# A mixer stage: attention steps with a second probability buffer and later transposes, and the recurrence's products on VectorE

## The chip, the cores and the metric

The kernel runs on one core of one Trainium2 chip. The metric is the device time of one execution in microseconds. The core has a matrix engine (TensorE, PE), a vector engine (VectorE, DVE), an engine for functions of one operand (ScalarE, ACT), a general engine (GpSimd, POOL), and SyncE, which issues most DMAs. Each works through its own queue in order; semaphores tie the queues together.

## The reference, cut to what matters

One decoder block over 512 tokens of width 1024: a mixer with two parallel groups of heads, then a channel mixer that retrieves experts. The change touches the mixer between its input projection and its output projection:

```python
def one_block(args):                       # differential attention, 4 heads, two maps j each
    s = jnp.einsum('bhjqd,bhjkd->bhjqk', qi, k) * scale
    s = jnp.where(mask, s, -jnp.inf)
    p = jax.nn.softmax(s, axis=-1)
    a = p[:, :, 0] - lam * p[:, :, 1]
    return jnp.einsum('bhqk,bhkv->bhqv', a, vf)

def step(state, inp):                      # HGRN2 recurrence, 4 heads, chunkwise
    q_, k_, v_, b_ = inp                   # b_: running sum of the log of the forget gate
    decay = jnp.exp(jnp.where(causal, b_[..., :, None, :] - b_[..., None, :, :], -jnp.inf))
    attn = jnp.einsum('bhtk,bhtsk,bhsk->bhts', q_, decay, k_)
    o_intra = jnp.einsum('bhts,bhsv->bhtv', attn, v_)
    o_inter = jnp.einsum('bhtk,bhkv->bhtv', q_ * jnp.exp(b_), state)
    ...
```

## The kernel before

The kernel is a row of stages with a barrier between them: input projection, `stage_mix`, `stage_join` (output projection and residual), selection, gates, experts. Everything that the diff touches lies in `stage_mix`. Its operands are in SBUF already; it starts no DMA.

The attention is worked through in 16 steps (`STEPS_A`), step n being head n // 4 and query tile n % 4, so a step has one to four key tiles of 128. A loop over n is written out for each engine, with 18 turns. In turn n

- TensorE forms the scores of step n (L943, and the causal mask by L946) into PSUM banks 2(n % 2) and the next, the product with the values of step n-2 (L955), then in turns 0 to 7 column sums of the modulation (L314) or in turns 8 to 17 eight level products of the recurrence in two groups (L930), and last the transposes of `mixed` of step n-1 (L973);
- VectorE takes the maxima of step n (L840), scales them into `nbias` (L842), and mixes step n-1: reciprocals of the sums and their factor (L850, L851), the first map scaled (L852) and the second added to it (L854), into `mixed`. In the turns of `ITEMS` it subtracts for one level of the recurrence (L862, L875, for the last item L866), and in turns 8 to 17 it copies two groups of level products under a mask (L830);
- ScalarE forms the exponentials of step n into `prob` (L768), copies out the attention of step n-2 (L774), copies the transposes of step n-1 into `mixedT` (L780), squares the attention (L783), and in the turns of `ITEMS` forms the exponentials of a level (L788, L789, L799, L800, L793, L794).

`prob` is one buffer, so exp(n) waits for mix(n-1) (`mixed_ready`); `nbias`, `Z`, `mixed`, `mixedT` and the score banks have two.

The recurrence is split into five levels (`LEVELS`): inside blocks of 8, and between halves of blocks of 16, 32, 64 and 128. For each level the exponentials `E` are multiplied by `kk` and `q` into `F` (L725, L726 for level 0; L736, L737 for the others, half a tile each), and so are those for the carried state (`"kb"`, L741, L742). GpSimd does this, each level as soon as its exponentials are there (`exp_ready`) and its slot of `F` is free (`level_done`). It then multiplies the output gate `hg` by its gain (L743). Ahead of all that it fills masks (L704 to L722).

Behind the loop TensorE transposes `F` slot 3 (L982), ScalarE copies that into `kbT` (L804), TensorE forms the chunk states (L990), VectorE carries them on (L894 to L900), and TensorE forms the recurrence's output (L1001, L1004). GpSimd normalizes the attention meanwhile (L749, L751).

Of the kernel before, what the change touches and what calls it, by code (L numbers as in the profile page):

```python
# [9 lines left out]
ALU = mybir.AluOpType  # L10
ACT = mybir.ActivationFunctionType
AX_X = mybir.AxisListType.X

P = 128
# [600 lines left out]
STEPS_A = HEADS * TT  # L615
LEVEL_AT = 8
LEVEL_END = LEVEL_AT + HEADS * len(LEVELS) // 2

ITEMS = {1: 0, 3: 1, 5: 2, 7: 3, 9: 4, 11: "kb"}
SLOT_E = (0, 0, 1, 0, 1)  # L620
# [3 lines left out]
def stage_mix(nc, a, m):  # L624
    with ExitStack() as own:
# [16 lines left out]
        prob = sb("prob", [P, 2, S])  # L642
# [59 lines left out]
        def _(pool):  # L702
# [21 lines left out]
            pool.wait_ge(exp_ready, 1)  # L724
            g.tensor_tensor(F[:, 0, :], E[:, 0, :], kk, ALU.mult).then_inc(f_ready, 1)  # L725
            g.tensor_tensor(F[:, 1, :], E[:, 1, :], q, ALU.mult).then_inc(f_ready, 1)  # L726
            for level in range(1, len(LEVELS)):
                h = LEVELS[level]
                pool.wait_ge(exp_ready, level + 1)
                if level == 3:  # L730
                    pool.wait_ge(level_done, HEADS)
                out = F[:, SLOT_F[level][0], :].rearrange("p (n c) -> p n c", c=2 * h)
                e = E[:, SLOT_E[level], :].rearrange("p (n c) -> p n c", c=2 * h)
                kv = kk.rearrange("p (n c) -> p n c", c=2 * h)
                qv = q.rearrange("p (n c) -> p n c", c=2 * h)
                g.tensor_tensor(out[:, :, 0:h], e[:, :, 0:h], kv[:, :, 0:h], ALU.mult).then_inc(f_ready, 1)  # L736
                g.tensor_tensor(out[:, :, h:], e[:, :, h:], qv[:, :, h:], ALU.mult).then_inc(f_ready, 1)  # L737

            pool.wait_ge(exp_ready, len(LEVELS) + 1)
            pool.wait_ge(level_done, 3 * HEADS)  # L740
            g.tensor_tensor(F[:, 2, :], E[:, 0, :], q, ALU.mult).then_inc(f_ready, 1)  # L741
            g.tensor_tensor(F[:, 3, :], E[:, 1, :], kk, ALU.mult).then_inc(f_ready, 1)  # L742
# [14 lines left out]
        def _(act):  # L757
# [3 lines left out]
            for n in range(STEPS_A + 2):  # L761
                if n < STEPS_A:
                    k = (n % TT + 1) * P
                    act.wait_ge(bias_ready, n + 1)
                    if n >= 1:
                        act.wait_ge(mixed_ready, n)
                    for j in range(2):
                        A(prob[:, j, 0:k], m.psum[2 * (n % 2) + j][:, 0:k], ACT.Exp, bias=nbias[:, n % 2, j:j + 1],  # L768
                          scale=QK ** -0.5, accum_out=Z[:, n % 2, j:j + 1]).then_inc(probs_ready, 1)
# [1361 lines left out]
```

## Time and profile before

| | |
|---|---|
| Time, median of 3 runs | 1952.97 us (1951.37 to 1954.81) |
| The profiled execution's own time | 1953.12 us |
| Its span | 1951.4 us |
| Mean granted TensorE clock | 0.945 |
| Busy in the span: TensorE, VectorE, ScalarE, GpSimd | 1796.0, 1182.1, 707.6, 672.1 us |
| `stage_mix`'s loop | 214.8 to 346.1 us |

Span is the time from the first to the last instruction. Times of instructions are counted from the span's start. A granted clock of 1.00 is 2.4 GHz, of 0.50 1.2 GHz. On TensorE the product of two fp32 operands shows as several records; "x8" counts records. "Idle before, releaser" in square brackets is how long the engine stood still before an instruction and what ended that. A difference between starts is often more telling than a duration, since the end of one instruction overlaps the start of the next.

### The profile page before, as it was taken

The page shows a single profiled execution, that of the slowest core. Times are in us where ns is not written, and L with a number is a line of the kernel's source. Part 1 is how long each engine was busy: PE and PEld are TensorE (multiplying, and loading weights), DVE is VectorE, ACT ScalarE, POOL GpSimd, SP SyncE. Part 2 cuts the span into 40 slices and gives each one's busy share as a digit, 9 for nine tenths or more (in the row PEclk, how much of TensorE's full clock was granted, in tenths as well). Part 3 has the DMA queues.
Part 4 walks back from the last instruction along what each step waited for, and adds up shares of the span by engine and source line. Part 5 has one row for each costly group of instructions (what it writes and reads, how often), then busy time and mean ns, then how long its engine had stood idle before and what let it go on. Part 6 is the DMA issues. An engine that isn't in the chain of part 4 may idle for free. (4 is left out here: it accounts for less than half of the span.)

```text
span 1951.4 us, 23199 instructions
## 1 busy us (share of the span) xinstructions
PE 1796.0 (92%) x8309; PEld 1482.8 (76%) x8309; DVE 1182.1 (61%) x2038; ACT 707.6 (36%) x1113; POOL 672.1 (34%) x486
## 2 busy tenths in 40 slices
PE   6999886777999689999998999999899999999996
PEld 6877564656777578888887888888688888888885
DVE  3766467734999945545553333333357887778776
ACT  3213343433332235555554223222233333333332
POOL 0000333203867642222221000000166776667750
PEclk8999767897999889999999999999999999999998
DMA  8563000312223234456556655555488988899985
GB/s 352 182 226 108 1 1 1 134 66 92 76 70 115 90 119 157 157 189 192 167 188 204 218 187 182 176 176 191 148 302 298 351 320 323 300 349 359 319 301 196
DMA packets 159708, 369.92 MB, mean 190 GB/s; under 512 B 16288, under 2 KB 78240, under 8 KB 156192
## 3 DMA queue, kind: packets, MB, share of 16 engines
q1 hardware_dynamic: 137120, 302.08, 44.4%
q0 software_dynamic: 22528, 67.19, 9.7%
q8 instruction: 20, 0.33, 0.1%
q14 instruction: 40, 0.33, 0.1%
HBM read 306.30 MB, written 62.91 MB: 189 GB/s over the span
## 5 line engine op out<-in xcount | busy, mean ns | idle before, releaser
L2064 PE MATMUL bank<-hl,actT 128*128 128x512 f32 x2304 | 524.5, 390 | 9.8 <-DVE actT L2004 9.8
L2064 PEld LDWEIGHTS bank<-hl,actT 128*128 128x128 f32 x2304 | 433.3, 188 | 101.0 <-DVE hl L1999 11.0
L1788 PE MATMUL bank<-actT,hl 128*128 128x512 f32 x1440 | 329.5, 391 | 6.8 <-DVE hl L1759 6.8
L1788 PEld LDWEIGHTS bank<-actT,hl 128*128 128x128 f32 x1440 | 272.3, 189 | 63.7 <-DVE hl L1759 7.0
L1644 PE MATMUL bank<-actT,hl 128*128 128x512 f32 x1152 | 275.5, 395 | 6.2 <-DVE hl L1603 6.2
L1644 PEld LDWEIGHTS bank<-actT,hl 128*128 128x128 f32 x1152 | 214.2, 189 | 48.7 <-DVE hl L1603 6.4
L1424 PE MATMUL bank<-actT,hl 128*128 128x512 f32 x864 | 212.3, 405 | 31.4 <-POOL hl L1270 28.1
L1961 ACT ACTIVATE hl<-v_raw 128x1024 fp32r<-128x1024 f32 x128 | 135.6, 1059 | 285.7 <-PE bank L2064 259.1
L1920 POOL DMA_INDIRECT rows<-in_v,own_index x65 | 83.6, 1286 | 422.8 <-POOLq L1684 351.9
L1424 PEld LDWEIGHTS bank<-actT,hl 128*128 128x128 f32 x864 | 167.3, 196 | 70.4 <-POOL hl L1270 18.5
L1999 DVE TENSOR_TENSOR hl<-v_raw,hl 128x1024 fp32r<-128x1024 f32 x128 | 157.1, 1227 | 90.1 <-ACT hl L1961 89.8
L1926 POOL DMA_INDIRECT own_act<-early_activations,own_at x128 | 180.6, 1411 | 39.1 <-issue 39.1
L1542 POOL TENSOR_TENSOR onehot<-first_hits,slotsT 128x512 f32<-128x512 bf16 x48 | 91.2, 1901 | 261.2 <-DVE first_hits L1610 261.2
L1768 DVE TENSOR_TENSOR kept_acts<-kept_acts,group_gates 128x384 f32<-128x384 f32 x60 | 33.5, 558 | 174.5 <-ACT kept_acts L1742 124.8
L1571 ACT ACTIVATE onehot<-first_hits,slotsT 128x128 f32<-128x128 bf16 x192 | 85.2, 515 | 78.7 <-DVE first_hits L1610 78.7
L1603 DVE TENSOR_TENSOR hl<-raw,hl 128x1024 fp32r<-128x1024 f32 x48 | 58.8, 1226 | 89.2 <-ACT hl L1557 89.2
L1270 POOL TENSOR_TENSOR hl<-raw,hl 128x1024 fp32r<-128x1024 f32 x32 | 82.0, 2564 | 81.3 <-ACT hl L1290 81.3
L1742 ACT ACTIVATE kept_acts<-bank 128x512 f32<-128x512 f32 x60 | 35.8, 597 | 201.8 <-PE bank L1788 201.8
L1759 DVE TENSOR_TENSOR hl<-raw,hl 128x1024 fp32r<-128x1024 f32 x60 | 73.3, 1226 | 55.7 <-ACT hl L1733 55.7
L1920 POOL DMA_INDIRECT raw<-in_v,own_index x63 | 77.6, 1232 | 54.8 <-DVE raw L2020 21.4
L1660 PEld LDWEIGHTS bank<-onehot 128*128 128x128 f32 x768 | 93.1, 191 | 3.7
L1660 PE MATMUL bank<-onehot 128*128 128x128 f32 x768 | 93.4, 275 | 0.0
(254 smaller groups left out, 2291.0 us busy)
## 6 DMA issues: line engine op xcount, KB each, us to landing
raw<-in_u SPq DMA_DIRECT2D x128, 512.0 KB, 3.8
v_raw<-in_v SPq DMA_DIRECT2D x128, 512.0 KB, 6.0
expert_gates<-gates SPq DMA_DIRECT2D x12, 2048.0 KB, 9.8
group_gates<-expert_gates SPq DMA_DIRECT2D x32, 768.0 KB, 6.2
acts_in<-early_activations SPq DMA_DIRECT2D x100, 192.0 KB, 4.9
wada<-in_w_ada SPq DMA_DIRECT2D x9, 2048.0 KB, 7.5
early_activations<-kept_acts SPq DMA_DIRECT2D x60, 256.0 KB, 2.2
early_activations<-gate_acts SPq DMA_DIRECT2D x48, 256.0 KB, 2.3
```

The costliest lines, as they stand in the source:

```text
L1270: g.tensor_tensor(hl[:, 1, u % m.split, :], raw[:, u, :], hl[:, 0, u % m.split, :].bitcast(F32), ALU.subtract).then_inc(m.unit_lo, 1)
L1424: last = nc.tensor.matmul(m.psum[u % 2][:], hl[:, x, u % m.split, kc * P:(kc + 1) * P], m.actT[:, z, kc, :], start=(kc == 0 and j == 0), s ...
L1542: nc.gpsimd.tensor_tensor(onehot1[:, b % BUFS, 0:pool_n, :].rearrange("p t k -> p k t"), hits[:, b % BUFS, :, 0:pool_n], slotsT[:, 2, n].u ...
L1571: last = A(onehot1[:, r % BUFS, u, :], hits[:, r % BUFS, :, u], ACT.Copy, scale=slotsT[:, 2, at:at + 1])
L1644: last = nc.tensor.matmul(m.psum[n % 2][:], hl[:, x, n % m.split, kc * P:(kc + 1) * P], m.actT[:, z, kc, :], start=(kc == 0 and j == 0), s ...
L1660: last = nc.tensor.matmul(chunk_bank(b, c)[:, k * NKEY:(k + 1) * NKEY], onehot1[:, b % BUFS, u, :], onehot2[:, b % BUFS, u, :], start=True ...
L1788: last = nc.tensor.matmul(m.psum[u % 2][:], hl[:, x, u % m.split, kc * P:(kc + 1) * P], m.actT[:, z, kc, :], start=(kc == 0 and j == 0), s ...
L1920: nc.gpsimd.indirect_dma_start(out=fetched[k % FETCH], out_offset=None, in_=rows_of_v, in_offset=bass.IndirectOffsetOnAxis(ap=m.own_index[ ...
L1926: nc.gpsimd.indirect_dma_start(out=own_act[:, k:k + 1], out_offset=None, in_=acts_of_u, in_offset=bass.IndirectOffsetOnAxis(ap=m.own_at[:, ...
L1961: A(v[:, 0, j, :], v_raw[:, j, :], ACT.Copy).then_inc(v_hi, 1)
L1999: V.tensor_tensor(v[:, 1, j, :], v_raw[:, j, :], v[:, 0, j, :].bitcast(F32), ALU.subtract).then_inc(v_lo, 1)
L2064: last = nc.tensor.matmul(bank(t, half)[:], w[:, x, j, t * P:(t + 1) * P], v[:, z, j, half * S:(half + 1) * S], start=(first and j == 0 an ...
```

## The change

`prob` becomes two buffers, and exp(n) waits for mix(n-2) instead of mix(n-1). TensorE transposes step n-2 instead of n-1 in turn n and forms the values' product of step n-3 instead of n-2; ScalarE's copies follow; the loop has 19 turns. The twelve products into `F` leave GpSimd's queue and go into VectorE's, at the turns that `PRODUCTS` lists, behind the mix and ahead of `ITEMS` and of the masked copies. GpSimd keeps the masks and, right behind them, the product of `hg` with its gain.

```diff
--- before.py
+++ after.py
@@ -613,10 +613,12 @@
 CHUNK = P
 NCH = S // CHUNK
 STEPS_A = HEADS * TT
+LAST = 3
 LEVEL_AT = 8
 LEVEL_END = LEVEL_AT + HEADS * len(LEVELS) // 2
 
 ITEMS = {1: 0, 3: 1, 5: 2, 7: 3, 9: 4, 11: "kb"}
+PRODUCTS = {2: (0,), 4: (1,), 6: (2,), 10: (3, 4), 14: ("kb",)}
 SLOT_E = (0, 0, 1, 0, 1)
 SLOT_F = ((0, 1), (2, 2), (3, 3), (0, 0), (1, 1))
 
@@ -639,7 +641,7 @@
         attnT = sb("attnT", [P, HEADS, S])
         kbT = sb("kbT", [P, NCH - 1, HEADS * HD])
         state = sb("state", [P, NCH - 1, HEADS * HD])
-        prob = sb("prob", [P, 2, S])
+        prob = sb("prob", [P, 2, 2, S])
         mixed = sb("mixed", [P, 2, S])
         mixedT = sb("mixedT", [P, 2, S])
         masks = sb("masks", [P, len(LEVELS), P])
@@ -721,25 +723,6 @@
                                                   pattern=[[2 * h, P // (2 * h)], [0, h]], channel_multiplier=-1))
             g.memset(attnT[:], 0.0).then_inc(masks_ready, 1)
 
-            pool.wait_ge(exp_ready, 1)
-            g.tensor_tensor(F[:, 0, :], E[:, 0, :], kk, ALU.mult).then_inc(f_ready, 1)
-            g.tensor_tensor(F[:, 1, :], E[:, 1, :], q, ALU.mult).then_inc(f_ready, 1)
-            for level in range(1, len(LEVELS)):
-                h = LEVELS[level]
-                pool.wait_ge(exp_ready, level + 1)
-                if level == 3:
-                    pool.wait_ge(level_done, HEADS)
-                out = F[:, SLOT_F[level][0], :].rearrange("p (n c) -> p n c", c=2 * h)
-                e = E[:, SLOT_E[level], :].rearrange("p (n c) -> p n c", c=2 * h)
-                kv = kk.rearrange("p (n c) -> p n c", c=2 * h)
-                qv = q.rearrange("p (n c) -> p n c", c=2 * h)
-                g.tensor_tensor(out[:, :, 0:h], e[:, :, 0:h], kv[:, :, 0:h], ALU.mult).then_inc(f_ready, 1)
-                g.tensor_tensor(out[:, :, h:], e[:, :, h:], qv[:, :, h:], ALU.mult).then_inc(f_ready, 1)
-
-            pool.wait_ge(exp_ready, len(LEVELS) + 1)
-            pool.wait_ge(level_done, 3 * HEADS)
-            g.tensor_tensor(F[:, 2, :], E[:, 0, :], q, ALU.mult).then_inc(f_ready, 1)
-            g.tensor_tensor(F[:, 3, :], E[:, 1, :], kk, ALU.mult).then_inc(f_ready, 1)
             g.tensor_tensor(hg.rearrange("p (n c) -> p n c", c=HD), hg.rearrange("p (n c) -> p n c", c=HD),
                             g_hgrn.unsqueeze(1).to_broadcast([P, TT * HEADS, HD]), ALU.mult).then_inc(hg_ready, 1)
 
@@ -758,28 +741,28 @@
             A = nc.scalar.activation
             act.wait_ge(lam_sums, 1)
             A(lams[:, 2:4], lams[:, 0:2], ACT.Exp).then_inc(lam_exps, 1)
-            for n in range(STEPS_A + 2):
+            for n in range(STEPS_A + LAST):
                 if n < STEPS_A:
                     k = (n % TT + 1) * P
                     act.wait_ge(bias_ready, n + 1)
-                    if n >= 1:
-                        act.wait_ge(mixed_ready, n)
+                    if n >= 2:
+                        act.wait_ge(mixed_ready, n - 1)
                     for j in range(2):
-                        A(prob[:, j, 0:k], m.psum[2 * (n % 2) + j][:, 0:k], ACT.Exp, bias=nbias[:, n % 2, j:j + 1],
+                        A(prob[:, n % 2, j, 0:k], m.psum[2 * (n % 2) + j][:, 0:k], ACT.Exp, bias=nbias[:, n % 2, j:j + 1],
                           scale=QK ** -0.5, accum_out=Z[:, n % 2, j:j + 1]).then_inc(probs_ready, 1)
-                if n >= 2:
-
-                    h, t = divmod(n - 2, TT)
-                    act.wait_ge(attn_out, n - 1)
+                if n >= 3:
+
+                    h, t = divmod(n - 3, TT)
+                    act.wait_ge(attn_out, n - 2)
                     A(cat[:, t, h * HD:(h + 1) * HD], m.psum[5][:, 0:HD], ACT.Copy).then_inc(attn_read, 1)
-                if 1 <= n <= STEPS_A:
-                    k = ((n - 1) % TT + 1) * P
-                    act.wait_ge(mixed_tr, n)
-                    if n >= 3:
-                        act.wait_ge(attn_out, n - 2)
-                    A(mixedT[:, (n - 1) % 2, 0:k], m.psum[4][:, 0:k], ACT.Copy).then_inc(mixedT_ready, 1)
-                if n >= 2:
-                    act.wait_ge(attn_read, n - 1)
+                if 2 <= n < STEPS_A + 2:
+                    k = ((n - 2) % TT + 1) * P
+                    act.wait_ge(mixed_tr, n - 1)
+                    if n >= 4:
+                        act.wait_ge(attn_out, n - 3)
+                    A(mixedT[:, n % 2, 0:k], m.psum[4][:, 0:k], ACT.Copy).then_inc(mixedT_ready, 1)
+                if n >= 3:
+                    act.wait_ge(attn_read, n - 2)
                     m.act.then(act, A(squared[:], cat[:, t, h * HD:(h + 1) * HD], ACT.Square,
                                       accum_out=ss[:, 0, t, h:h + 1]))
                 item = ITEMS.get(n)
@@ -832,7 +815,29 @@
                                       m.psum[6 + u % 2][:].rearrange("p (n c) -> p n c", c=P)
                                       ).then_inc(level_copied, 1)
 
-            for n in range(STEPS_A + 2):
+            def products(level):
+                if level == 0:
+                    dve.wait_ge(exp_ready, 1)
+                    V.tensor_tensor(F[:, 0, :], E[:, 0, :], kk, ALU.mult).then_inc(f_ready, 1)
+                    V.tensor_tensor(F[:, 1, :], E[:, 1, :], q, ALU.mult).then_inc(f_ready, 1)
+                elif level == "kb":
+                    dve.wait_ge(exp_ready, len(LEVELS) + 1)
+                    dve.wait_ge(level_done, 3 * HEADS)
+                    V.tensor_tensor(F[:, 2, :], E[:, 0, :], q, ALU.mult).then_inc(f_ready, 1)
+                    V.tensor_tensor(F[:, 3, :], E[:, 1, :], kk, ALU.mult).then_inc(f_ready, 1)
+                else:
+                    h = LEVELS[level]
+                    dve.wait_ge(exp_ready, level + 1)
+                    if level == 3:
+                        dve.wait_ge(level_done, HEADS)
+                    out = F[:, SLOT_F[level][0], :].rearrange("p (n c) -> p n c", c=2 * h)
+                    e = E[:, SLOT_E[level], :].rearrange("p (n c) -> p n c", c=2 * h)
+                    kv = kk.rearrange("p (n c) -> p n c", c=2 * h)
+                    qv = q.rearrange("p (n c) -> p n c", c=2 * h)
+                    V.tensor_tensor(out[:, :, 0:h], e[:, :, 0:h], kv[:, :, 0:h], ALU.mult).then_inc(f_ready, 1)
+                    V.tensor_tensor(out[:, :, h:], e[:, :, h:], qv[:, :, h:], ALU.mult).then_inc(f_ready, 1)
+
+            for n in range(STEPS_A + LAST):
                 if n < STEPS_A:
                     k = (n % TT + 1) * P
                     dve.wait_ge(scores, n + 1)
@@ -849,10 +854,12 @@
                         dve.wait_ge(mixed_tr, o - 1)
                     m.dve.then(dve, V.reciprocal(rz[:, o % 2, :], Z[:, o % 2, :]))
                     m.dve.then(dve, V.tensor_scalar(rz[:, o % 2, 1:2], rz[:, o % 2, 1:2], lams[:, 0:1], None, ALU.mult))
-                    m.dve.then(dve, V.tensor_scalar(mixed[:, o % 2, 0:k], prob[:, 0, 0:k], rz[:, o % 2, 0:1], None,
+                    m.dve.then(dve, V.tensor_scalar(mixed[:, o % 2, 0:k], prob[:, o % 2, 0, 0:k], rz[:, o % 2, 0:1], None,
                                                     ALU.mult))
-                    V.scalar_tensor_tensor(mixed[:, o % 2, 0:k], prob[:, 1, 0:k], rz[:, o % 2, 1:2],
+                    V.scalar_tensor_tensor(mixed[:, o % 2, 0:k], prob[:, o % 2, 1, 0:k], rz[:, o % 2, 1:2],
                                            mixed[:, o % 2, 0:k], ALU.mult, ALU.add).then_inc(mixed_ready, 1)
+                for level in PRODUCTS.get(n, ()):
+                    products(level)
                 item = ITEMS.get(n)
                 if item is not None:
                     if item == 0:
@@ -931,7 +938,7 @@
                                         F[:, SLOT_F[level][1], at], start=True, stop=True)
                     last.then_inc(level_done, 1)
 
-            for n in range(STEPS_A + 2):
+            for n in range(STEPS_A + LAST):
                 if n < STEPS_A:
                     h, t = divmod(n, TT)
                     k = (t + 1) * P
@@ -945,8 +952,8 @@
 
                         last = T.matmul(bank[:, t * P:k], m.ident_bf[:], negmask[:], start=False, stop=True)
                     last.then_inc(scores, 1)
-                if n >= 2:
-                    o = n - 2
+                if n >= 3:
+                    o = n - 3
                     h, t = divmod(o, TT)
                     pe.wait_ge(mixedT_ready, o + 1)
                     if o >= 1:
@@ -964,8 +971,8 @@
                     if n == LEVEL_AT:
                         pe.wait_ge(mod_read, 1)
                     level_matmuls(n)
-                if 1 <= n <= STEPS_A:
-                    o = n - 1
+                if 2 <= n < STEPS_A + 2:
+                    o = n - 2
                     pe.wait_ge(mixed_ready, o + 1)
                     if o >= 1:
                         pe.wait_ge(mixedT_ready, o)
```

## Rows read from the trace of the kernel before

**Rows 1.** The two parts of the mixer's loop: each engine's busy time, granted clock, DMA

```profile
core 0: us, PE busy (x) PEld busy (x) DVE busy (x) ACT busy (x) POOL busy (x), PEclk, DMA share, GB/s
...
214.00:273.00 59.00, 48.58 (x154) 31.38 (x154) 32.98 (x61) 22.06 (x60) 25.53 (x25) 0.51 0.00 1
...
273.00:346.00 73.00, 53.64 (x286) 39.79 (x286) 53.85 (x83) 27.67 (x86) 24.14 (x7) 0.79 0.00 1
```

**Rows 2.** Who waited for whom, 214 to 346 us: total, times, longest

```profile
ACT prob L768 <- DVE mixed L854: 72.1, 14, 12.9
...
PE bank L973 <- DVE mixed L854: 27.0, 8, 9.8
```

**Rows 3.** TensorE in order of time: start, us, instruction, idle before

```profile
214.78 0.79 PE L943 MATMUL bank<-projT 64*128 64x128 f32 x2 [3.50 <-POOL negmask L705]
...
216.53 1.81 PE L314 MATMUL bank<-ones,ada_sums 128*128 128x1 f32 x8
...
248.05 1.09 PE L973 MATMUL bank<-ident,mixed 128*128 128x128 f32 x4
...
249.07 1.22 PE L943 MATMUL bank<-projT 64*128 64x256 f32 x2
...
251.67 2.02 PE L955 MATMUL bank<-projN,mixedT 128*128 128x128 f32 x8
...
253.49 1.71 PE L314 MATMUL bank<-ones,ada_sums 128*128 128x1 f32 x8
...
276.21 3.57 PE L930 MATMUL bank<-F 128*128 128x128 f32 x16
...
282.57 1.95 PE L930 MATMUL bank<-F 128*128 128x128 f32 x16
...
284.56 0.91 PE L943 MATMUL bank<-projT 64*128 64x384 f32 x2
...
346.12 1.04 PE L982 MATMUL bank<-ident,F 128*128 128x128 f32 x8
```

**Rows 4.** VectorE in order of time, same columns

```profile
229.48 4.70 DVE L854 SCALAR_TENSOR_TENSOR mixed<-prob,rz,mixed 128x256 f32<-128x256 f32 x1
...
245.33 0.62 DVE L840 TENSOR_REDUCE nbias<-bank 128x1 f32<-128x128 f32 x2 [0.68 <-PE bank L946]
...
247.04 0.75 DVE L854 SCALAR_TENSOR_TENSOR mixed<-prob,rz,mixed 128x512 f32<-128x512 f32 x1
...
253.96 2.28 DVE L875 TENSOR_TENSOR wada<-projT 128x2048 f32<-128x2048 f32 x1
...
269.13 1.42 DVE L840 TENSOR_REDUCE nbias<-bank 128x1 f32<-128x512 f32 x2 [5.22 <-PE bank L946]
...
286.06 1.36 DVE L830 COPY_PREDICATED attnT<-masks,bank 128x512 f32<-128x512 uint32 x2
...
324.10 4.59 DVE L854 SCALAR_TENSOR_TENSOR mixed<-prob,rz,mixed 128x256 f32<-128x256 f32 x1
...
339.90 0.75 DVE L854 SCALAR_TENSOR_TENSOR mixed<-prob,rz,mixed 128x512 f32<-128x512 f32 x1
```

**Rows 5.** GpSimd in order of time

```profile
220.02 1.80 POOL L722 MEMSET attnT<- 128x2048 f32 x1
...
229.40 4.50 POOL L725 TENSOR_TENSOR F<-wada 128x2048 f32<-128x2048 f32 x1 [7.57 <-ACT wada L789]
...
323.87 4.54 POOL L743 TENSOR_TENSOR projN<-projN,small 128x2048 f32<-128x2048 f32 x1
```

**Rows 6.** ScalarE in order of time

```profile
225.46 1.91 ACT L788 ACTIVATE wada<-wada 128x2048 f32<-128x2048 f32 x1 [0.95 <-DVE wada L862]
...
346.84 1.07 ACT L804 ACTIVATE kbT<-bank 128x512 f32<-128x512 f32 x2
```

**Rows 7.** Stretches of 8 us, columns as in Rows 1

```profile
286.00:294.00 8.00, 2.93 (x21) 2.18 (x19) 7.83 (x10) 2.12 (x2) 8.00 (x4) 0.95 0.00 0
...
326.00:334.00 8.00, 5.25 (x9) 1.80 (x10) 4.03 (x4) 1.97 (x8) 2.42 (x1) 0.50 0.00 0
```

## The prediction

> **What bounds the kernel now.** I read the page for the whole, then the stretches of the stage that the diff touches, its list of waits, and each engine's instructions in order of time. The attention loop runs from 214.8 us [rows 3] to 346.1 us, where the first transpose for the carried state starts [rows 3]. In neither half is an engine full: of 59 us TensorE has 48.6 busy at a clock of 0.51, VectorE 33.0; of the following 73 us TensorE 53.6, VectorE 53.9 [rows 1]. So the loop is bound by a chain. The list of waits names it: ScalarE's exponentials wait 72.1 us for `mixed`, the transposes on TensorE 27.0 us [rows 2]. Inside a step, mix(n-1) on VectorE releases the transposes of n-1, TensorE then does scores(n+1), VectorE their maxima, then mix(n): products, transposes and mixing stand in one line. No DMA moves (share 0.00 in [rows 1]), so nothing prefetched absorbs a gain; what the loop loses the span should lose.
>
> The second cost is between GpSimd and VectorE. A mix of 256 columns takes 4.70 and 4.59 us where one of 512 takes 0.75 [rows 4]; the first ends with GpSimd's product that began at 229.40 and took 4.50, the second covers the product of 323.87 [rows 4, 5]. Summed over nine such instructions from 229 to 329 us, each less its undisturbed duration, this is about 21 us; the first and the last of the nine stand in [rows 4].
>
> **The change, part by part.** *Second probability buffer.* exp(n) no longer waits for mix(n-1), only for mix(n-2). ScalarE is 22 of 59 and 28 of 73 us busy [rows 1], so this costs nothing. *Transposes one step later.* TensorE does transposes(n-2), whose `mixed` is ready a step earlier, so scores(n+1) are no longer behind mix(n-1). The drain has one more step. *Products to VectorE.* It gains 4 instructions over 2048 columns and 8 over 1024. The nearest row is its subtraction of the same size, 2.28 us [rows 4], 2.2 to the next start; a half I put at 1.15. Sum 4 x 2.2 + 8 x 1.15 = 18.0 us, at worst 20.5 if strided halves cost 10% more and starts don't overlap. GpSimd loses 12 products. The stalls of 21 us go, and 18 us of own work come.
>
> *What stays on GpSimd* is the gain product of 4.54 us on `hg`. It has no wait of its own, and its predecessor ends at 221.8 [rows 5], so it moves to 221.8 to 226.4. There VectorE is about to scale the maxima of step 1 and mix step 0. By the blocked rows above it stands until 226.4: 4.4 us lost, at the start.
>
> The Trainium skill ("Perfetto Trace Analysis", Optimizing Scalar/DVE Operations) speaks against this part: VectorE and GpSimd share a read port, "so offloading operations between those two might not help". Here the trace shows the sharing, and what it would make of the time is the third rival below.
>
> Now the queues, with durations by key tiles. VectorE: two maxima 0.65 to 1.45 us (0.62 and 1.42 in [rows 4]), scaling 0.1, mix 1.06, 1.24, 1.44, 1.64 (the last instruction alone is 0.75 [rows 4]), subtraction 2.2, a masked copy 0.66 (two 1.36 [rows 4]). TensorE at 1.2 GHz: scores 1.75 (214.78 to 216.53), 2.60 (249.07 to 251.67), so 3.45 and 4.31 for three and four tiles; values 0.53 to 1.82, modulation sums 1.65, transposes 0.41 to 1.02, eight level products 1.7 [rows 3]. At 2.4 GHz eight level products take 0.92 (sixteen 1.95) and scores 0.98 to 2.28 (three tiles, one map of two, 0.91) [rows 3].
>
> *Start to max(3).* The stall ends 226.5, rest of mix(0) 0.7 and subtraction 2.2 give 229.4; max(2) and mix(1) run while ScalarE needs 3.9 for its two exponentials (1.91 each [rows 6]), to 233.5; products 4.4 give 237.9.
>
> *To scores(8).* max(3) 1.55, exp(3) 1.4, ScalarE's two copies 0.6 lead to values(1) at 241.5; with sums(4) and transposes(2) 3.4, scores(5) start at 244.9. From there TensorE is full: scores 5 to 8 12.1, values 2 to 4 3.7, three sums 5.0, transposes 3 to 5 2.0, sum 22.9: scores(8) end at 267.8. Before they ended at about 275.0 (the level products follow at 276.2 [rows 3]). Gain so far 7.2.
>
> *To the last mix.* values(5), the first eight level products at half clock (the clock rose within 3.57 us of them before [rows 3]) and scores(9) lead to max(9) at 274.1. Now VectorE is the full engine: maxima 9 to 15 8.5, mixes 8 to 15 10.8, two subtractions 4.4, products 4.6 + 4.4, 14 copies 9.2 = 41.9, plus 2.3 of waits for scores: mix(15) ends at 318.3. Before it ended at 340.65 [rows 4]. Gain 22.3.
>
> *Tail.* mix(15) to the end of the last values is 5.8 us. Before, level products hid ScalarE's last copy, square and root (with a table load) before `kbT`; after, values(15) come last, and that cover is gone: 2.8 us to the first `kbT` instead of 1.3. It lands at 326.9, before at 347.4 (346.84 plus half of 1.07 [rows 6]): 20.5 less. Behind it both kernels are the same.
>
> The same bookkeeping laid over the kernel before gives 345.5 for that copy, 1.9 short of the row: starts and waits that I round away. I take 1.6 off for that: **18.9 us**. The profiled execution took 1953.1 (span 1951.4), the median is 1952.97; the forecast is 1953.1 - 18.9 = 1934.2.
>
> **Rivals.**
> *(a) An earlier full clock.* If denser work lifts TensorE's clock already among the steps that carry modulation sums (about 247 us), scores and level products halve from there; then VectorE's queue alone remains, `kbT` lands near 320.5, gain 27: 1926. Against it: the clock read 0.51 in that half [rows 1] even through 5.4 us without an idle moment (248.05 to 253.49 [rows 3]).
> *(b) Slower: the clock stays at half.* The clock was 0.95 in 286 to 294, where TensorE was busy for 2.9 of 8 us, and 0.50 in 326 to 334, behind the longest stall of VectorE [rows 4, 7]: it falls behind standing still, and it rose in level products [rows 3]. After the change these come in pairs of bursts with VectorE's copies and products between them. Were it at 1.2 GHz throughout, TensorE's queue alone is scores 48.4, values 18.8, sums 13.2, level products 34, transposes 11.5 = 126 us; from 214.8, with 6.5 of waits at the start and 2.8 behind, `kbT` lands at 350.1 plus 1.6, 4.3 later than before: 1957. It decides from where more than about four fifths of the level steps run at half clock. A half clock in half of them gives a gain near 8: 1945. For it: my queues leave TensorE idle 3.1 us before level product 6 (products 3 and 4 stand ahead of copies on VectorE); the shortest idle time after which I find a half clock is 3.50 us [rows 3].
>
> *(c) The move between engines gains nothing.* One port serves both, so the products on VectorE cost what the stalls cost and only the later transposes pay. With the change's order but products on GpSimd, the same bookkeeping lands `kbT` at 331.5 plus 1.6: gain 14.3: 1939. The skill's sentence quoted above would have it so. Against it: 18.0 us of work stands against 21 us of stalls plus GpSimd's own 39 us of products (12, the first of them 4.50 [rows 5]), on which copies and levels waited.
>
> **How the numbers follow.** Forecast 1934.2, with its own range 1930 to 1938 (products 2.5 us dearer, one more cold stretch 3; or the stall at 222 half hidden), 0.58. (a) 0.11. (c) 0.14. (b) with half clock in part, 1942 to 1950, 0.12; (b) in full 0.03, and 0.02 for a cost at the edge of no change that I have not named. 1927 to 1942 leaves out (b) and part of (a), 0.2 in all. Beyond 0.2% (3.9 us), which a measurement here can tell from no change: faster 0.94 (forecast, (a), (c) and nearly all of (b) in part), same 0.03, slower 0.03.
>
> **What would show it.** VectorE's mixes at their undisturbed durations after 230 us, one stall at 222 to 226; twelve products of 2.3 and 1.2 us on VectorE; exponentials' wait for `mixed` nearly gone; max(9) near 274 and mix(15) near 319; VectorE 80% busy or more between; the clock at 1.0 there; the last 20 us of the stage as before, 1.5 longer. Wrong is the forecast if the clock digits in the level steps stay at 5, if the products take 3 us or more, or if a later stage gives the time back.

## The result and the profile after

The changed kernel took 1934.43 us (median of 4 runs, 1933.3 to 1937.54) against 1952.17 us: a ratio of 0.991, 95% interval 0.9892 to 0.9927. In a second series it took 1933.72 us against 1952.28 us, 0.9907 (0.9891 to 0.9924). The forecast was 1934.2.

The profiled execution (1937.54 us, the slowest of its series) has a span of 1935.8 us. Its mixer stage began 1.8 us later than before (first scores at 216.55 us, not 214.78), so I count from there. Two stretches of the loop, with the columns of [rows 1]:

```profile
214.00:273.00 59.00, 52.25 (x169) 34.48 (x170) 44.95 (x79) 25.18 (x66) 11.02 (x20) 0.52 0.00 1
...
273.00:328.00 55.00, 47.47 (x271) 37.36 (x271) 43.93 (x81) 23.54 (x75) 0.00 (x0) 0.83 0.00 1
```

The loop's second part is 55 us long, not 73, at nearly the same clock (0.83 against 0.79 in [rows 1]), with VectorE busy for 43.9 of it, and no GpSimd work. The waits in 214 to 346 us (columns as in [rows 2]):

```profile
ACT prob L751 <- issue: 26.6, 7, 6.7
...
ACT prob L751 <- DVE nbias L847: 17.0, 5, 7.9
...
ACT mixedT L763 <- PE bank L980: 10.6, 8, 3.3
```

The two waits of [rows 2] for `mixed` are gone from the list. VectorE in order of time, first the stall at the start, then the products, a maximum and the last mix:

```profile
223.81 4.34 DVE L847 TENSOR_SCALAR nbias<-nbias 128x2 f32<-128x2 f32 x1
...
235.29 2.29 DVE L821 TENSOR_TENSOR F<-wada 128x2048 f32<-128x2048 f32 x1 [1.43 <-ACT wada L772]
...
239.69 1.41 DVE L845 TENSOR_REDUCE nbias<-bank 128x1 f32<-128x512 f32 x2
...
247.23 1.22 DVE L837 TENSOR_TENSOR F<-wada 128x1024 f32<-128x1024 f32 x1
...
276.38 0.88 DVE L845 TENSOR_REDUCE nbias<-bank 128x1 f32<-128x256 f32 x2 [1.39 <-PE bank L953]
...
319.56 0.75 DVE L859 SCALAR_TENSOR_TENSOR mixed<-prob,rz,mixed 128x512 f32<-128x512 f32 x1
```

```profile
223.62 4.50 POOL L726 TENSOR_TENSOR projN<-projN,small 128x2048 f32<-128x2048 f32 x1
```

L847 is the scaling of two numbers a partition that else takes 0.17 us. It stood for 4.34 us beside GpSimd's gain product. All 16 mixes have their undisturbed durations (the last, 0.75, as in [rows 4]). TensorE at the same places as in [rows 3]:

```profile
216.55 0.79 PE L950 MATMUL bank<-projT 64*128 64x128 f32 x2 [3.50 <-POOL negmask L707]
...
246.68 1.22 PE L950 MATMUL bank<-projT 64*128 64x256 f32 x2
...
269.24 1.17 PE L962 MATMUL bank<-projN,mixedT 128*128 128x128 f32 x4
...
289.75 3.75 PE L937 MATMUL bank<-F 128*128 128x128 f32 x16 [2.91 <-DVE attnT L813]
...
319.07 3.50 PE L937 MATMUL bank<-F 128*128 128x128 f32 x16
...
328.32 1.04 PE L989 MATMUL bank<-ident,F 128*128 128x128 f32 x8
...
331.94 4.47 PE L997 MATMUL bank<-projN,kbT 128*128 128x128 f32 x24
```

For all kernels below I read three places from their traces, in us from the first scores: the end of the last mix, the end of the first copy into `kbT`, and the start of the next stage on VectorE (`gcol`), called the length of the stage below. The fourth column is the span behind that, the same code in all. The next stage's first row, before and after:

```profile
366.65 0.37 DVE L1097 TENSOR_TENSOR gcol<-mod,gains 128x8 f32<-128x8 f32 x2 [0.55 <-PEq L625]
```

```profile
351.97 0.37 DVE L1104 TENSOR_TENSOR gcol<-mod,gains 128x8 f32<-128x8 f32 x2 [0.55 <-PEq L627]
```

| kernel | last mix | kbT | next stage | rest of span | median time |
|---|---|---|---|---|---|
| before | 125.9 | 132.6 | 151.9 | 1584.8 | 1952.2 to 1953.0 |
| changed | 103.8 | 114.8 | 135.4 | 1583.8 | 1934.4 |
| changed, second series | 103.8 | 113.7 | 133.0 | 1582.4 | 1933.7 |
| order only | 107.3 | 116.9 | 136.2 | 1582.0 | 1936.3 |
| products only | 110.2 | 118.8 | 138.1 | 1585.7 | 1935.7 |
| buffer only | 126.5 | 132.7 | 152.0 | 1585.7 | 1953.2 |
| change with one buffer | 106.6 | 118.3 | 138.9 | 1584.8 | 1937.7 |
| gain product late | 98.1 | 107.2 | 126.5 | 1582.6 | 1928.0 |
| and kbT before the root | 99.7 | 109.3 | 130.2 | 1583.9 | 1929.4 |
| and two groups of sums ahead | 98.0 | 107.5 | 128.4 | 1583.8 | 1931.6 |
| a fourth of the sums | 99.5 | 108.6 | 127.8 | 1584.5 | 1930.4 |
| gain late, copies first | 102.4 | 113.9 | 133.2 | 1581.0 | 1931.0 |
| gain late, drain reordered | 99.6 | 109.2 | 130.3 | 1583.7 | 1930.3 |
| both of these | 102.5 | 112.4 | 133.6 | 1583.8 | 1933.7 |

The rest of the span scatters over 4.7 us with the same code, so a single execution says more by its stage than by its time. The stage is one profile per kernel, and it scatters too: 2.4 us between the two profiles of the changed kernel, with the last mix at 103.8 both times. The kernels that share a series were compared with the same runs of the kernel before.

### The profile page after: what moved, and what is told of

It is laid out like the page before. It is cut to its first block and busy times, and to the rows that moved or that the text cites. A ratio compares the mean times of both kernels' runs of the same rounds, so it can differ in the third digit from the quotient of the medians.

```text
span 1935.8 us, 23199 instructions
## 1 busy us (share of the span) xinstructions
PE 1797.4 (93%) x8309; PEld 1487.3 (77%) x8309; DVE 1181.4 (61%) x2050; ACT 707.9 (37%) x1113; POOL 634.3 (33%) x474
## 5 line engine op out<-in xcount | busy, mean ns | idle before, releaser
L1431 PE MATMUL bank<-actT,hl 128*128 128x512 f32 x864 | 214.3, 408 | 30.1 <-POOL hl L1277 26.8
L1277 POOL TENSOR_TENSOR hl<-raw,hl 128x1024 fp32r<-128x1024 f32 x32 | 86.4, 2700 | 80.6 <-ACT hl L1297 80.6
```

The lines of the kernel that those rows point to most:

```text
L1277: g.tensor_tensor(hl[:, 1, u % m.split, :], raw[:, u, :], hl[:, 0, u % m.split, :].bitcast(F32), ALU.subtract).then_inc(m.unit_lo, 1)
L1431: last = nc.tensor.matmul(m.psum[u % 2][:], hl[:, x, u % m.split, kc * P:(kc + 1) * P], m.actT[:, z, kc, :], start=(kc == 0 and j == 0), s ...
```

## Experiments

### Which half of the change pays

Order only: the changed kernel with the products back in GpSimd's queue.

```diff
-                for level in PRODUCTS.get(n, ()):
-                    products(level)
...
+            pool.wait_ge(exp_ready, 1)
+            g.tensor_tensor(F[:, 0, :], E[:, 0, :], kk, ALU.mult).then_inc(f_ready, 1)
...
```

> The later transposes and the second probability buffer as in the changed kernel, the twelve products still on GpSimd. The queues laid out as in the prediction land the first kbT 14.3 us earlier than before: about 1938 us, against 1952 before and 1934 for the whole change. The rival that the move between engines gains nothing expects it within 1 us of the whole change, about 1934 to 1935. If the order gives little by itself: above 1945. In the profile: VectorE's mixes of steps 9 and 13 still stretched to 2 us and more beside GpSimd's products.

It took 1936.3 us, ratio 0.9916 (0.9896 to 0.9936). VectorE's stalls are all still there, beside GpSimd's products (VectorE, then GpSimd):

```profile
234.00 4.26 DVE L866 TENSOR_SCALAR nbias<-nbias 128x2 f32<-128x2 f32 x1
...
305.83 4.23 DVE L876 TENSOR_SCALAR mixed<-prob,rz 128x256 f32<-128x256 f32 x1
...
310.10 4.60 DVE L878 SCALAR_TENSOR_TENSOR mixed<-prob,rz,mixed 128x256 f32<-128x256 f32 x1
```

```profile
305.41 4.49 POOL L744 TENSOR_TENSOR F<-wada 128x2048 f32<-128x2048 f32 x1
```

Ten stretched instructions lose 23.3 us in all, more than the 21.3 of before, and the stage is still 15.7 us shorter. A stall hurt before because TensorE stood behind each mix (27.0 us [rows 2]); with the transposes a step later no wait for `mixed` is left in its list. Its level products wait 11.3 us for VectorE's masked copies instead.

Products only: the kernel before, with the products in VectorE's queue (the cut shows the added lines; the same twelve leave GpSimd's queue).

```diff
+PRODUCTS = {2: (0,), 4: (1,), 6: (2,), 10: (3, 4), 14: ("kb",)}
...
+                for level in PRODUCTS.get(n, ()):
+                    products(level)
                 item = ITEMS.get(n)
```

> The twelve products on VectorE, the attention steps as in the kernel before (one probability buffer, transposes of the step before, 18 turns). The laid-out queues give 16 us less than before, about 1936: each half of the change alone would take most of the gain, since either takes the long stalls off the chain. The rival (the move gains nothing) expects 1952, or more, since VectorE's 18 us of products then stand in the chain of every step. In between, 1940 to 1948, if the chain's own length matters more than the laid-out queues say.

It took 1935.72 us, ratio 0.9907 (0.989 to 0.9923); the stage lost 13.8 us where 16 was laid out. What is left of the chain:

```profile
ACT prob L750 <- DVE mixed L858: 55.7, 14, 8.6
...
PE bank L979 <- DVE mixed L858: 9.6, 8, 4.4
```

TensorE's transposes wait 9.6 us for `mixed` instead of 27.0 [rows 2]. By VectorE's own time the move brought nothing: 17.9 us of products and 3.9 of one stall (its first mix beside GpSimd's gain product) stand where 21.3 us of stalls stood. What changed is where they stand: the products lie outside the mixes that TensorE waits for.

So each half alone brings most of what both bring, and they don't add: 15.7 and 13.8 us against 16.5 to 18.9 together (the two profiles of the changed kernel). Both shorten the same wait, that of TensorE behind a stretched mix.

By time alone these kernels and the changed one can't be told apart. The last mix, which depends least on TensorE's clock in the drain, stands in order: 107.3 us with order only, 110.2 with products only, 103.8 twice with both.

### What the second buffer is worth

Buffer only: two probability buffers in the kernel before, exponentials of step n waiting for the mix of n-2 (the cut shows the wait alone).

```diff
-                    if n >= 1:
-                        act.wait_ge(mixed_ready, n)
+                    if n >= 2:
+                        act.wait_ge(mixed_ready, n - 1)
```

> Only the second probability buffer in the kernel before: exponentials of step n wait for the mix of n-2, everything else unchanged. Theory: the exponentials never stood last in the chain (TensorE waited for the mix, the mix for the maxima), so no gain, 1952 within 2 us, though the list of waits loses its 72 us of exponentials waiting for mixed. Rival: the buffer is what decouples the engines: 1940 or less.

1953.24 us, ratio 1.0004 (0.9994 to 1.0013). The chain is untouched (mix, transposes, scores, maxima):

```profile
265.04 0.69 PE L973 MATMUL bank<-ident,mixed 128*128 128x128 f32 x2 [2.83 <-DVE mixed L854]
...
270.20 1.42 DVE L840 TENSOR_REDUCE nbias<-bank 128x1 f32<-128x512 f32 x2 [5.22 <-PE bank L946]
```

```profile
PE bank L973 <- DVE mixed L854: 28.1, 9, 9.8
```

The exponentials no longer wait for `mixed`, and nothing came of it. The largest wait of a list, 72.1 us in [rows 2], was worth nothing by itself.

One buffer: the whole change, with `prob` and its wait as in the kernel before.

> The whole change but with one probability buffer: the exponentials of step n again wait for the mix of n-1. Theory: with the transposes later the exponentials now stand between two mixes, so this costs: the laid-out queues give 7 us above the whole change, about 1941, with VectorE idle ahead of the reciprocals. Rival: the buffer is worth nothing here either: 1934 to 1935.

1937.74 us, ratio 0.9918 (0.9902 to 0.9935). The stage took 138.9 us against 135.4 and 133.0, and the last mix ends 2.8 us later: the buffer is worth 3 to 6 us of the stage here, where 7 was laid out. By time alone that isn't resolved, the intervals overlap. The exponentials wait again:

```profile
ACT prob L751 <- DVE mixed L859: 52.8, 13, 8.6
...
PE bank L962 <- ACT mixedT L763: 9.9, 7, 3.5
```

The second buffer only pays once the transposes are later. That an exponential is last in the line between two mixes only then is how I read it; the waits agree.

### The gain product

Gain late: the changed kernel, with a wait that keeps GpSimd's product until the last mix is done.

```diff
+            pool.wait_ge(mixed_ready, STEPS_A)
             g.tensor_tensor(hg.rearrange(...), hg.rearrange(...), ..., ALU.mult).then_inc(hg_ready, 1)
```

> The changed kernel, but GpSimd's gain product on hg waits until the last mix is done. Theory: the 4.34 us for which VectorE stood at its scaling of step 1 go; TensorE then comes to scores(8) some 4 us earlier, and the stage from its first scores to the next stage takes 131.5 to 132.5 us instead of 135.4: about 1930.5 against 1934.4. The product itself is hidden beside the last level products and the table load. Rival: the first stall is hidden anyway, since TensorE at half clock is the full engine in turns 4 to 8: the stage stays within 1 us of 135.4.

1928.03 us, ratio 0.9883 (0.9863 to 0.9903). The scaling of step 1 takes 0.17 us again, and no instruction of VectorE's loop is stretched:

```profile
221.38 0.17 DVE L848 TENSOR_SCALAR nbias<-nbias 128x2 f32<-128x2 f32 x1
...
263.85 3.09 PE L938 MATMUL bank<-F 128*128 128x128 f32 x16
```

The level products begin 49.4 us behind the first scores, in the changed kernel 53.9 (270.44 - 216.55): 4.5 us, the stall. The last mix is 5.7 us earlier. The expectation was exceeded: the stage is 126.5 us where 131.5 to 132.5 was expected. Its 8.9 us over the first profile of the changed kernel hold more than the stall: the clock, below.

This stall also fits with how little the move of the products adds once the transposes are later, where VectorE is the fullest engine of order only (48.0 of 55 us busy from 273 to 328 us, TensorE 40.8). Order only lost 23.3 us of VectorE's time to stalls. The changed kernel spends 17.9 us on products (4 at 2.2 from start to start, 8 at 1.13) and 4.2 on the one stall: 22.1. With the gain product out of the way it is 17.9. In the kernel before the same sum would have promised nothing for the move, and the move was worth 13.8 us there.

### The drain

kbT before the root: gain late, and in ScalarE's queue the three copies into `kbT` ahead of the root with its table load.

```diff
-            A(ss[:, 0], ss[:, 0], ACT.Sqrt, ...).then_inc(roots, 1)
             for n in range(NCH - 1):
                 act.wait_ge(kb_tr, n + 1)
                 A(kbT[:, n, :], m.psum[n % 2][:], ACT.Copy).then_inc(kbT_ready, 1)
+            A(ss[:, 0], ss[:, 0], ACT.Sqrt, ...).then_inc(roots, 1)
```

> As gain_late, and ScalarE copies kbT before it takes the root with its table load. Theory: the drain's uncovered 1.6 us (table load and root ahead of kbT) goes, TensorE no longer stands 2.1 us ahead of its last transpose, and its clock stays up for the state products (3.1 us for 24 instead of 4.5): the stage is 1.5 to 3 us shorter than in gain_late. Rival: GpSimd's normalization of the attention, which waits for the root, is last there, and nothing is gained.

1929.4 us, ratio 0.9877 (0.9861 to 0.9894): no different from gain late by time, and the stage is 3.7 us longer instead of 1.5 to 3 shorter. `kbT` did come 1.5 us sooner behind the last values' product (1.4 us, in gain late 2.9). The expected gain from a warm clock was not to be had, since the 24 state products ran at full clock in gain late as well (3.13 us). And VectorE takes over the first state only here:

```profile
328.72 0.25 DVE L894 RECIPROCAL ss<-ss 128x16 f32<-128x16 f32 x1 [5.95 <-ACT ss L788]
...
329.00 0.69 DVE L902 COPY state<-bank 128x512 f32<-128x512 f32 x1
```

The reciprocal of the attention's roots stands ahead of the states in VectorE's queue, and it now waits for a root that comes later. The copies were made earlier and the wait moved one queue on. Neither theory had that: the rival was right that nothing is gained, for another reason. About 2 us of the difference between the two stages arose earlier, ahead of `kbT`, where turn 16's level products took 3.52 us at half clock and in gain late 1.95.

Drain: the reciprocal goes behind the three states as well.

```diff
-            inverse_norms(0)
             for n in range(NCH - 1):
                 dve.wait_ge(kv_done, n + 1)
...
+            inverse_norms(0)
             def sum_squares(t):
```

> As gain_kbt, and VectorE takes the reciprocal of the attention's roots behind the three chunk states instead of ahead of them. Theory: in gain_kbt the chunk states stood behind that reciprocal (VectorE idle 5.95 us until ScalarE's root), so the gain from copying kbT first was lost in VectorE's queue; now the first state follows the first state product, and from the first kbT to the next stage takes 17.5 to 18.5 us instead of 20.9 (gain_kbt) or 19.3 (gain_late). Rival: GpSimd's normalization, which starts 4 us later, ends last: no gain, 20 us or more.

1930.26 us, ratio 0.9877 (0.9861 to 0.9894), 21.1 us from `kbT` to the next stage: the rival. The states come at once, but GpSimd's normalization starts only at 331.04 and now lies beside VectorE's:

```profile
331.04 1.04 POOL L733 TENSOR_TENSOR rows<-rows,ss 128x512 f32<-128x512 f32 x1 [10.71 <-DVE ss L894]
...
339.88 1.59 POOL L735 TENSOR_TENSOR rows<-rows,small 128x512 f32<-128x512 f32 x1
...
341.55 1.37 POOL L695 TENSOR_TENSOR rows<-rows,ss 128x512 f32<-128x512 f32 x1
```

```profile
338.94 1.41 DVE L697 TENSOR_TENSOR rows<-rows,projN 128x512 f32<-128x512 f32 x1
...
340.38 1.63 DVE L695 TENSOR_TENSOR rows<-rows,ss 128x512 f32<-128x512 f32 x1
...
343.50 1.63 DVE L695 TENSOR_TENSOR rows<-rows,ss 128x512 f32<-128x512 f32 x1
```

VectorE's six operations of 0.69 us take 7.9 us together (337.97 to 345.86), since five meet GpSimd's products. The stall of VectorE beside GpSimd came back in another place.

### TensorE's clock and the 2.9 us wait

A fourth of the sums: the changed kernel with one modulation column a turn.

> The changed kernel with one column sum a turn instead of four (24 of the 32 modulation columns are left out), which takes 1.2 us of TensorE's work out of each of turns 0 to 7. Theory: TensorE's queue at half clock sets turns 4 to 8, so the first level product comes 6 to 8 us earlier and the stage ends 4 to 6 us earlier, about 1929. The prediction's rival (a) says besides that the clock rises among these denser steps: granted clock above 0.6 between the start of scores(2) and the first level product, and then 10 us or more; else it stays at 0.50.

One execution, 1930.38 us, stage 127.8 us. The first level product came 3.9 us earlier (50.0 us behind the first scores), not 6 to 8: it then waited 0.54 us for VectorE. The clock stayed at half until the first level products, as in the changed kernel itself, where TensorE was busy for three whole stretches (changed kernel, then this one, columns as in [rows 1]):

```profile
246.00:254.00 8.00, 8.00 (x29) 5.68 (x29) 7.60 (x13) 4.51 (x17) 0.00 (x0) 0.50 0.00 0
...
254.00:262.00 8.00, 8.00 (x25) 4.73 (x23) 4.68 (x9) 4.33 (x12) 0.00 (x0) 0.50 0.00 0
...
262.00:270.00 8.00, 8.00 (x27) 5.01 (x26) 4.79 (x8) 2.18 (x8) 0.00 (x0) 0.50 0.01 2
```

```profile
246.00:254.00 8.00, 7.72 (x22) 4.29 (x23) 6.79 (x11) 4.77 (x18) 0.00 (x0) 0.50 0.01 2
...
254.00:262.00 8.00, 8.00 (x24) 4.37 (x23) 5.78 (x11) 3.02 (x10) 0.00 (x0) 0.50 0.00 0
```

Rival (a) is out: in 24 us in which TensorE of the changed kernel shows no idle moment the clock never rose; it rose within level products. With fewer sums the stage is 5 to 8 us shorter (one profile against two), of which some 4 stand at the last mix: TensorE's queue at half clock is the limit in turns 4 to 8, as laid out, until VectorE's takes over.

Copies first: gain late, and the masked copies ahead of products and subtraction.

```diff
+                if n == LEVEL_AT:
+                    dve.wait_ge(masks_ready, 2)
+                if LEVEL_AT <= n < LEVEL_END:
+                    level_copies(n)
                 for level in PRODUCTS.get(n, ()):
                     products(level)
...
-                if n == LEVEL_AT:
-                    dve.wait_ge(masks_ready, 2)
-                if LEVEL_AT <= n < LEVEL_END:
-                    level_copies(n)
```

> As gain_late, and in turns 8 to 17 VectorE makes its two masked copies before products and subtraction. Theory: TensorE's waits of 2.9 and 2.3 us for copies (turns 11 and 15) go, so the clock stays at 1.0 from turn 9 to the end of the loop in each execution, and the stage takes 124 to 127 us each time, where gain_late took 126.5 with a clock of 0.82 to 0.97 in these turns. The laid-out queues say otherwise: VectorE then waits for level products behind the mix, and the stage is 2 to 3 us longer than gain_late. In both cases no TensorE wait above 2 us between turns 9 and 16.

1930.97 us, ratio 0.9895 (0.9877 to 0.9912); stage 133.2 us. The expectation of both sides, no wait of TensorE above 2 us, was wrong:

```profile
287.86 1.22 PE L963 MATMUL bank<-projN,mixedT 128*128 128x128 f32 x4 [3.74 <-ACT mixedT L764]
...
314.76 1.22 PE L963 MATMUL bank<-projN,mixedT 128*128 128x128 f32 x4 [4.23 <-ACT mixedT L764]
```

The wait for copies went and a longer one for `mixedT` came, whose copy stands in ScalarE's queue behind the exponentials of the next maxima. Those maxima come behind VectorE's four products in either order and are no later for it (69.7 us behind the first scores, in the drain variant, whose loop is that of gain late, 69.4). The time is lost in turn 13, where VectorE, as the laid-out queues had it, waits for level products behind the mix:

```profile
299.48 0.73 DVE L814 COPY_PREDICATED attnT<-masks,bank 128x512 f32<-128x512 uint32 x1 [2.65 <-PE bank L938]
```

The copies wait 5.6 us for level products in 262 to 320 us, in the drain variant 2.5. The last mix, 102.4 us, is 4.3 later than in gain late, and 2.7 to 2.8 later than in the two drain variants. The laid-out queues had said 2 to 3; the wish to keep the clock up was the wrong reason to overrule them.

Copies first with the reordered drain:

> copies_first and drain together: the two gains are in different parts of the stage and add up, if both are there: stage 122.5 to 126 us, time 1923 to 1928. If copies ahead cost as the laid-out queues say: 127 to 128.

1933.72 us, ratio 0.9904 (0.9887 to 0.992), stage 133.6 us. Neither gain is there, so nothing adds up.

Sums ahead: kbT before the root, and two groups of sums before the first scores.

> As gain_kbt, and the first two of the eight groups of modulation sums stand ahead of the first scores, where TensorE waits 3.5 us for GpSimd's mask; the others move two turns earlier. Theory: TensorE is the full engine in turns 5 to 8, so scores(8) come 3.3 us earlier; of that 0 to 3 us reach the end, since VectorE is the full engine behind it: stage 127.5 to 130.5 us. Rival: nothing reaches the end, within 0.5 us of gain_kbt.

1931.56 us, ratio 0.9889 (0.9872 to 0.9905): no gain. The idle time that the sums should fill was too short:

```profile
215.86 3.04 PE L314 MATMUL bank<-ones,ada_sums 128*128 128x1 f32 x16 [2.85 <-PEq L398]
```

They start 2.85 us into it and delay the first scores to 5.8 us behind the last product of the stage ahead, where it was 3.5. Counted from that product's end the stage takes 134.2 us, in the kernel without this edit 133.7.

The changed kernel again:

> The changed kernel itself once more, for its scatter and a second profile. Theory: behind VectorE's four products of turn 10 TensorE stands 2.9 us; whether its clock is at half behind that differs from one execution to the next. The stage is 135.4 us again if it is, about 132 if it isn't; the time 1931 to 1935.

It took 1933.72 us, stage 133.0 us. The level products behind VectorE's four products of turn 10, in this profile and in that of gain late:

```profile
287.17 3.76 PE L937 MATMUL bank<-F 128*128 128x128 f32 x16 [2.90 <-DVE attnT L813]
```

```profile
282.25 2.95 PE L938 MATMUL bank<-F 128*128 128x128 f32 x16 [2.91 <-DVE attnT L814]
```

TensorE idles 2.90 to 2.93 us ahead of them. The sixteen records then take 3.75 us (half clock) in seven of the eight profiles with this order of products (the changed kernel twice, and five variants), and 2.95 in one, that of gain late. Its stage of 126.5 us is a lucky one: the last mix stands at 98.1, against 99.6 and 99.7 with the same loop in the two drain variants, so about 1.5 us of its gain is chance. Most of that was there before the wait. The first level products of turn 8 took 3.09 us there and 3.78 in the drain variants, and the next ones began 55.0 us behind the first scores instead of 56.2 and 56.3. And the profile is that of the fastest of its four executions (1925.21 us, median 1928.03).

The expectation for this kernel, 135.4 if cold and 132 if not, wasn't met: it was cold and took 133.0. The last mix is the same as in the first profile, so turn 11's clock didn't decide. What differed came behind it: turn 16's level products took 1.95 us instead of 3.50 (with that `kbT` is 1.1 us earlier), and the 24 state products behind a 2.1 us wait took 3.13 us instead of 4.47, as in the kernel before:

```profile
347.96 3.13 PE L990 MATMUL bank<-projN,kbT 128*128 128x128 f32 x24
```

## Why the prediction was right

Counted from the first scores, the steps of the sum against the trace:

| place | laid out | measured |
|---|---|---|
| max(3) begins | 23.1 | 23.1 |
| scores(5) begin | 30.1 | 30.1 |
| scores(8) end | 53.0 | 52.7 |
| max(9) begins | 59.3 | 59.8 |
| last mix ends | 103.5 | 103.8 |
| last values end | 109.3 | 111.8 |
| first kbT, with 1.6 added | 113.7 | 114.8 (113.7 in the second profile) |
| stage, against before | -18.9 | -16.5 (-18.9) |

The forecast of the time, 1934.2 us against 1934.4, is closer than its working deserves. The profiled execution took 1937.5 us, and its span is 15.6 us shorter than before where 18.9 was laid out; the second profile's stage is 18.9 us shorter. The four executions spread over 4.2 us.

*The chain as the bound* held: buffer only left it alone and gained nothing; order only, products only and the change with one buffer shortened it. *The products' price* of 18.0 us was 17.9. *The stall of 4.4 us at the start* was 4.2 and came where it was put; gain late gave it back. *VectorE as the full engine from max(9)* held to 0.3 us over 44 us; it was 80% busy, as forecast. *TensorE full at half clock before that* held too: fewer sums shortened it. One sign of the forecast didn't come: TensorE's clock was to stand at 1.0 in the level steps, and it was 0.83.

*The cover lost in the drain* (2.8 us instead of 1.3) was right, but what the clock does around and behind the last mix was missing: in the first profile level products of turn 16 took 3.50 us, not 1.95, behind the waits of turns 15 and 16 (2.26 and 1.10 us), and the state products 4.47, not 3.13. In the second profile only those of turn 15 were slow (3.75 us). The 1.6 us that I took off for rounding was needed in full there, and in no step before; it covered a term that I hadn't named, so that part of the hit is luck. The half clock behind level product 6 (3 us of my range) happened: the wait ahead of it was 2.91 us where I had 3.1. It cost the last mix nothing that shows, which came where it was put.

*Rival (c)*, that the move between engines gains nothing beside the order, was closer than its chance of 0.14. The laid-out difference was 4.6 us, measured 3.5 at the last mix, 0.8 to 3.2 in the stage, and in time not resolvable (1936.3 against 1934.4 and 1933.7). Its reason fits as well, beside the later transposes: products on VectorE plus the remaining stall (22.1 us) cost nearly what the stalls cost (23.3). Without the later transposes it fails: the amounts are much the same (21.8 against 21.3), and the move alone made the stage 13.8 us shorter.

The Trainium skill's sentence on offloading between these two engines ("Perfetto Trace Analysis", Optimizing Scalar/DVE Operations), that it might not help, agrees with this case only for the move on top of the later transposes, 3.5 us at the last mix. It doesn't for the move alone (products only), nor with the gain product out of the way (gain late, 9.2 us over order only at the last mix, about 1.5 of them chance).

*Rivals (a) and (b)* are decided by the clock of the level steps, 0.83: neither up early nor half throughout.

The stage explains all of the difference: 16.5 us shorter in the first profile, the rest of the span 0.9, the stage's later beginning -1.8, together 15.6, the difference of the two spans.

## What to carry to other kernels

Lay the queues out instruction by instruction from the trace's durations, and check the same bookkeeping against the kernel before: that gave each place up to the last mix to 0.5 us, and where a theory of mine overruled it (copies first) it was right and the theory wrong. Behind the last mix it was 1.4 to 2.7 us short; what TensorE's clock does there wasn't in it.

Two cures for one stall hardly add. Whether work moved from GpSimd to VectorE pays depends on what stands behind the stalls and on what GpSimd work is left beside VectorE, so put the last GpSimd product where VectorE idles. The three variants that do only that, or that and a reordered drain, have ratios of 0.9883 (0.9863 to 0.9903), 0.9877 and 0.9877; they can't be told apart, and by time their intervals overlap with that of the changed kernel. Their last mixes, 98.1 to 99.7 us against 103.8 twice, are apart. A long entry in the list of waits (72 us) can be worth nothing; ask who waits for the waiting engine.

## What the hardware showed that I had not expected

TensorE's clock fell behind waits shorter than any I had found a half clock behind. That was 3.50 us [rows 3] in the kernel before. Here it is 2.90 to 2.93 us in seven profiles of eight, and once (changed kernel, second series) 2.26 us, with all sixteen records at half clock. The shortest is 1.76 us, in products only, where the granted clock reads 1.00 in the 2 us ahead of the wait and 0.50 behind it:

```profile
311.71 3.75 PE L937 MATMUL bank<-F 128*128 128x128 f32 x16 [2.26 <-DVE attnT L813]
```

```profile
319.82 3.75 PE L936 MATMUL bank<-F 128*128 128x128 f32 x16 [1.76 <-DVE attnT L812]
```

In the first profile of the changed kernel the records behind the 2.26 us took 2.46 us, in the variant with a fourth of the sums 2.02, which is full clock. Behind the wait of 2.1 us ahead of the state products the clock was full in five profiles of seven and half in two. So the outcome of one wait differed between executions. Why isn't settled; no run varied the wait alone.
